# A hybrid attention block on one core: values of three heads projected ahead of the head loop, and each head's last steps placed among the next head's first two weight tiles

## Chip, core and metric

The kernel runs on one core of a Trainium2 chip. The engines are TensorE (PE, with PEld for its weight loads), VectorE (DVE), ScalarE (ACT), GpSimd (POOL) and SyncE (SP), which issues all DMA transfers here. The metric is the device time of one execution in microseconds.

## What is computed

A sequence of 1024 rows of width 1024 is normalised and projected by one weight matrix of 4352 columns. The columns feed three groups of heads; their gated outputs go through one output projection, the residual is added, and the rows are normalised again.

```python
hn = rmsnorm(h, g_norm[l]);  proj = hn @ w_in[l]
aq, ak, av, ag, bq, bk, bv, bg, mq, mg = jnp.split(proj, IN_SPLITS, axis=-1)
# A: 8 query heads of 64, 2 key heads, window of two 64-row chunks, sinks
# B: 4 heads, causal by chunk: softmax(q0 k0) - lam * softmax(q1 k1), times v (128 wide), then rmsnorm
# M: 4 heads of 128 against 256 normalised memory rows
gated = concatenate([a_out * silu(ag), b_out * silu(bg), m_out * silu(mg)])
h = h + gated @ w_out[l];  return rmsnorm(h, g_final)
```

## The kernel before

**Arithmetic.** Every fp32 operand of a product is split into a high part (`hi`, by an ACT copy) and a rest (`lo`, by a subtraction on POOL or DVE). `product` (L1495 to L1499) issues three matmuls, hi by hi, hi by lo and lo by hi. The small A products and all transposes are single fp32 matmuls; a transpose is a matmul against `ident`.

**Stages.** A prologue turns and normalises the memory and the input rows into `x_hi` and `x_lo`, makes keys and values of the memory, and projects the shared keys and values of group A. Then come four heads, written as one list of steps, `HEAD` (L121), and for the last head `LAST`. The output projection ends the kernel.

**A head.** Its eight weight tiles (`TILES`: bk, bq, bv, aq, ag, mq, mg, bg) are 1024 x 128 each. `project(w, s, q)` is a quarter of one half of a tile: six matmuls of 512 columns into bank `acc[:, s]`; four quarters make the half, so a tile takes 48 matmuls. `evacuate(w, s)` empties the bank: for bk with four ACT copies and two DVE subtractions, for bq with two and two, for bv and aq with one DVE instruction, for a gate (ag, mg, bg) with an ACT tanh and a DVE product. The table `BETWEEN` says which attention steps stand behind which quarter; (7, 0, 3) is the last quarter of the first half of tile 7.

**Order and waits.** All five engines walk the same list, each taking its own part of every step, and an engine does its parts strictly in that order. Semaphores join them. A half may start when the bank that it writes was evacuated: `project_quarter` (L1685) waits for `acc_free` of two halves earlier. Transposes go through two banks (`trans`), outputs of attention through one (`mixo`), scores through three (`score`).

**The end of group B in a head.** The squares of the head's output are summed on PE (`b_squares`); `b_finish(s)` takes the root on ACT (L857, which needs another table of functions) and on DVE the reciprocal (L1400) and a product (L1402); `b_gate` (L1410) multiplies by the gates. SP then stores the gates to DRAM (`spill`, L513).

**The values of a head.** Tile bv is projected turned, 128 value columns by 1024 rows, copied to `b_out`, turned back by eight transposes in `v_spread` (L1707), and split to `v_hi` and `v_lo`.

Of the kernel before, what the change touches and what calls it, by code (L numbers as in the profile page):

```python
# [45 lines left out]
TILES = [("bk", BK, True), ("bq", BQ, True), ("bv", BV, False), ("aq", AQ, True),  # L46
         ("ag", AG, True), ("mq", MQ, False), ("mg", MG, False), ("bg", BG, False)]
NT = len(TILES)
BUSY = (14, 2, 2)
PRE_TILES = 10  # L50
MEM_TILES = 8
PRE_RAW = 4
# [5 lines left out]
BETWEEN = {  # L58
    (2, 0, 2): [("b_scores", 0, 0)],
    (2, 0, 3): [("b_scores", 1, 0), ("b_combine", 0)],  # L60
    (2, 1, 1): [("b_combine", 1)],
# [30 lines left out]
}  # L92

def numbered(*events):

    return {key: n for n, key in enumerate(events)}


def head_steps(between):

    out = [("start",)]  # L110
    for w in range(NT):
        out.append(("weights", w + 1))
        for s in range(2):
            for q in range(4):
                out.append(("project", w, s, q))
                if q == 3:
                    out.append(("evacuate", w, s))
                out += between.get((w, s, q), [])
    return out


HEAD = head_steps(BETWEEN)

BETWEEN_LAST = {
    **BETWEEN,
    (7, 1, 0): BETWEEN[(7, 1, 0)] + [("mix_first", 0)],
# [8 lines left out]
LAST = head_steps(BETWEEN_LAST)  # L135
# [15 lines left out]
def score_units():  # L151

    out = []
    for s in HEAD:
# [15 lines left out]
T_AT = numbered(*[s for s in HEAD if s[0] in ("v_spread", "b_spread", "m_spread", "a_spread", "b_squares")])  # L170

T_SPLIT = numbered(*[s for s in HEAD if s[0] in ("v_spread", "b_spread", "m_spread")])

PT_AT = numbered(*[s for s in HEAD if s[0] in ("b_spread", "m_spread")])
PT_MIX = numbered(*[s for s in HEAD if s[0] in ("b_spread", "m_spread")])
assert list(PT_MIX) == [(s[0][0] + "_spread",) + s[1:] for s in HEAD if s[0] in ("b_mix", "m_mix")]
O_AT = numbered(*[s[:2] for s in HEAD
                  if s[0] in ("m_mix", "a_mix") or (s[0] == "b_mix" and s[2] == s[1])])
NS, NTB, NPT, NO = len(S_AT), len(T_AT), len(PT_AT), len(O_AT)
# [5 lines left out]

def build(nc, x, mem, w_in, g_norm, a_sinks, lq1, lk1, lq2, lk2, subln_g, g_mem, w_mem_kv, w_out,
          g_final, y):
    mixed = nc.dram_tensor("mixed", (SPILL_TILES * P, SEQ), F32).ap()

# [6 lines left out]
    mixed_v = mixed.rearrange("(j p) s -> p j s", p=P)  # L196

# [16 lines left out]
    with ctx:  # L214
# [65 lines left out]
        q_m_hi, q_m_lo = q_b[:, 0, :], q_b[:, 1, :]  # L280
        bv_t = b_out[:, 0:SEQ]
        squares = logits[:, 0, 0, :]
# [56 lines left out]
        mixo = ctx.enter_context(nc.psum_tensor("mixo", [P, HALF], F32))  # L339
        y_acc = [score[:, 0, :], score[:, 1, :], trans[:, 0, :], trans[:, 1, :]]  # L340
# [13 lines left out]
        mv_made = sem("mv_made")  # L354
        mem_w_full = [sem(f"mem_w_full{n}") for n in range(2, MEM_TILES)]
# [90 lines left out]
        def raw_at(w, h):  # L446

            return h * (NT // 2 * 32) + 32 * ((PRE_RAW + w) // 2 + 1)


        @block.sync
        def _(sp):
# [49 lines left out]
            for w in range(2):  # L502
                sp.wait_ge(w_lo_done, PRE_TILES - 1 + w)
                load_tile(w_in_v, w, TILES[w][1], 4 * DK)

            def load_head_tile(w, h):

                name, col, two = TILES[w % NT]
                step = DK if two else P
                sp.wait_ge(w_lo_done, at(w - 2, h, NT, PRE_TILES))  # L510
                load_tile(w_in_v, w % 2, h * step + (col + (step if w >= NT else 0)), 4 * DK if two else None)
# [10 lines left out]
            with sp.Fori(0, HEADS - 1) as h:  # L522
                for w in range(2, NT + 2):
                    load_head_tile(w, h)
                for g in "amb":
                    spill(g, h)
            for w in range(2, NT):
                load_head_tile(w, HEADS - 1)

            n_tiles = PRE_TILES + NT * HEADS  # L530

            def load_wo(j):
# [4 lines left out]
                dst = wo_raw[j - 1] if j else w_raw[:, 0, :]  # L537
# [3 lines left out]
                for c, row in enumerate((first, second)):  # L541
                    sp.dma_start(dst[c * DK:(c + 1) * DK, :], w_out_v[row:row + DK, :])\
                      .then_inc(wo_full[j - 1] if j else raw_full[0], 16)
# [11 lines left out]
            for g in "abm":  # L555
                sp.wait_ge(spilled[g], 16 * H)
            sp.wait_ge(mkv_lo, 2 * HEADS)
            load_mix(0, 0)
            sp.wait_ge(s_full, at(S_AT[("b", 7, 1, 1)], H, NS))
            load_wo(1)  # L560
            load_wo(2)
            sp.wait_ge(s_free_dve, len(S_BY_DVE) * HEADS)
            load_mix(1, 1)
            sp.wait_ge(s_full, NS * HEADS)
            load_wo(3)
            sp.wait_ge(acc_full, PRE_ACC + 2 * NT * HEADS)
# [3 lines left out]
            sp.wait_ge(t_free, PRE_T + NTB * HEADS)  # L570
# [923 lines left out]
        def _(pe):  # L1494
# [161 lines left out]
            for v in range(2, 4):  # L1656
                spread_shared(v)
# [252 lines left out]
```

## Time and profile before

| | us |
|---|---|
| median of 3 runs | 703.88 |
| lowest, highest | 703.14, 704.38 |
| the profiled execution | 703.16 |
| its span in the trace | 701.4 |
| PE busy | 691.6 (99%) |
| DVE, ACT, POOL busy | 417.4, 313.2, 231.2 |

A row of the chronological view gives start, duration, engine, line, operation, output and inputs, shape, count, and in brackets the idle time before it and who ended it. Ends of matmuls are modelled and overlap the next one's start, so what PE needs for a matmul is read from start to start. The four heads begin near 65, 190, 314 and 439 us; the output projection runs from 563 us to 696 us.

### The profile page before, as it was taken

How to read it: one execution, taken by the hardware profiler on the slowest of the kernel's cores; microseconds unless marked ns; L12 is line 12 of the kernel's file. 1: busy time of each engine (PE TensorE's matmuls, PEld its weight loads, DVE VectorE, ACT ScalarE, POOL GpSimd, SP SyncE). 2: the span in 40 equal slices, each digit the busy share in tenths (PEclk: the TensorE clock that was granted, in tenths of full speed). 3: DMA queues.
4: the chain of work that ended last, by engine and by line, in shares of the span. 5: the costliest groups of instructions: out<-in, count | busy, mean ns of one | idle time of the engine just before them, and what ended most of it. 6: DMA issues, size and time to landing. Idle time of an engine off the chain costs nothing.

```text
span 701.4 us, 11592 instructions
## 1 busy us (share of the span) xinstructions
PE 691.6 (99%) x3933; PEld 579.2 (83%) x3933; DVE 417.4 (60%) x916; ACT 313.2 (45%) x733; POOL 231.2 (33%) x204
## 2 busy tenths in 40 slices
PE   8999999999999999999999999999999999999996
PEld 8888888888888888888888888888888887888885
DVE  6785246766854666675366667635667786433332
ACT  7763434456543444564344556434464654122200
POOL 5723132234323214433221434323243543222310
PEclk9999999999999999999999999999999999999999
DMA  9921211020052102005211110521140285514210
GB/s 298 310 61 34 57 40 52 1 61 2 1 160 51 55 7 54 8 1 150 61 31 31 32 30 1 150 61 31 31 124 6 60 274 154 158 60 131 84 55 36
DMA packets 79157, 52.73 MB, mean 75 GB/s; under 512 B 36080, under 2 KB 71936, under 8 KB 79104
## 3 DMA queue, kind: packets, MB, share of 16 engines
q1 hardware_dynamic: 79104, 52.06, 26.0%
q8 instruction: 29, 0.48, 0.3%
q14 instruction: 24, 0.20, 0.1%
HBM read 43.14 MB, written 8.91 MB: 74 GB/s over the span
## 4 chain that ended last, share of the span: by engine, by line
PE 92%; DVE 5%; ACT 1%; issue 1%; DVEq 0%; POOL 0%; ACTq 0%; POOLq 0%
PE acc L1497 17%; PE acc L1498 17%; PE acc L1499 17%; PE score L1497 4%; PE score L1498 4%; PE score L1499 4%; PE trans L1498 3%; PE trans L1497 3%; PE trans L1499 3%; PE score L1702 2%; PE score L1704 2%; PE trans L1722 2%; PE mixo L1498 2%; DVE logits L1400 2%; PE mixo L1499 2%; PE mixo L1497 2%
## 5 line engine op out<-in xcount | busy, mean ns | idle before, releaser
L1497 PE MATMUL acc<-x_hi,w_hi 128*128 128x512 f32 x512 | 204.1, 399 | 0.2 <-DVE gates L1265 0.2
L1498 PE MATMUL acc<-x_lo,w_hi 128*128 128x512 f32 x512 | 200.2, 391 | 0.0
L1499 PE MATMUL acc<-x_hi,w_lo 128*128 128x512 f32 x512 | 199.9, 390 | 0.0
L942 POOL TENSOR_TENSOR w_lo<-w_raw,w_hi 128x512 fp32r<-128x512 f32 x66 | 84.9, 1307 | 174.2 <-ACT w_hi L610 156.4
L1499 PEld LDWEIGHTS acc<-x_hi,w_lo 128*128 128x128 f32 x512 | 96.2, 188 | 20.8
L1497 PEld LDWEIGHTS acc<-x_hi,w_hi 128*128 128x128 f32 x512 | 96.3, 188 | 19.3 <-issue 1.4
L1498 PEld LDWEIGHTS acc<-x_lo,w_hi 128*128 128x128 f32 x512 | 96.4, 188 | 16.7
L789 ACT ACTIVATE logits<-logits,stats_b 128x128 f32<-128x128 f32 (+7 forms) x64 | 49.2, 770 | 50.5 <-DVE stats_b L1294 50.5
L1286 DVE CUSTOM_DVE_ANT_0 logits<-score,b_bias 128x384 f32<-128x384 f32 (+5 forms) x96 | 49.8, 554 | 23.2 <-PE score L1704 22.6
L798 ACT ACTIVATE p_hi<-trans 128x512 fp32r<-128x512 f32 (+1 forms) x56 | 30.8, 565 | 63.4 <-PE trans L1722 42.1
L1313 DVE TENSOR_TENSOR p_lo<-trans,p_hi 128x512 fp32r<-128x512 f32 (+1 forms) x56 | 35.8, 651 | 33.6 <-ACT p_hi L798 33.2
L990 POOL TENSOR_SCALAR logits<-logits,stats_b,small 128x128 f32<-128x128 f32 (+7 forms) x32 | 26.3, 823 | 68.1 <-DVE stats_b L1303 68.1
L1306 DVE SCALAR_TENSOR_TENSOR logits<-logits,stats_b 128x128 f32<-128x128 f32 (+7 forms) x32 | 26.2, 818 | 35.4 <-POOL logits L990 35.4
L610 ACT ACTIVATE w_hi<-w_raw 128x512 fp32r<-128x512 f32 x64 | 36.7, 622 | 13.6 <-DMA w_raw<-in_w_in 5.3
L835 ACT ACTIVATE a_band<-a_band,stats_a 128x128 f32<-128x128 f32 x64 | 24.9, 391 | 34.5 <-DVE stats_a L1367 34.2
L965 POOL TENSOR_TENSOR mix_lo<-mix_raw,mix_hi 128x1152 fp32r<-128x1152 f32 (+1 forms) x8 | 18.1, 2260 | 65.6 <-ACT mix_hi L732 64.3
L732 ACT ACTIVATE mix_hi<-mix_raw 128x1152 fp32r<-128x1152 f32 (+2 forms) x10 | 9.6, 971 | 63.2 <-PE score L1499 33.6
L1497 PE MATMUL score<-wo,mix_hi 128*128 128x512 f32 x88 | 34.7, 394 | 0.7 <-DVE wo L1207 0.7
L1498 PE MATMUL score<-wo,mix_hi 128*128 128x512 f32 x88 | 34.3, 389 | 0.0
L1499 PE MATMUL score<-wo,mix_lo 128*128 128x512 f32 x88 | 34.2, 389 | 0.0
L1497 PE MATMUL trans<-wo,mix_hi 128*128 128x512 f32 x88 | 34.2, 389 | 0.0
L1498 PE MATMUL trans<-wo,mix_hi 128*128 128x512 f32 x88 | 34.2, 389 | 0.0
(254 smaller groups left out, 1395.5 us busy)
## 6 DMA issues: line engine op xcount, KB each, us to landing
w_raw<-in_w_in SPq DMA_DIRECT2D x68, 256.0 KB, 3.4
mixed<-gates SPq DMA_DIRECT2D x9, 512.0 KB, 4.2
mix_raw<-mixed SPq DMA_DIRECT2D x8, 576.0 KB, 5.9
wo_raw<-in_w_out SPq DMA_DIRECT2D x8, 512.0 KB, 7.1
x_res<-in_x SPq DMA_DIRECT2D x8, 512.0 KB, 3.3
out_y<-y_row SPq DMA_DIRECT2D x16, 256.0 KB, 2.1
logits<-in_x SPq DMA_DIRECT2D x4, 512.0 KB, 8.0
wo_raw<-in_w_out SPq DMA_DIRECT2D x6, 256.0 KB, 5.9
```

What stands on the lines that cost most here:

```text
L610: act.activation(w_hi[:, slot, cols], w_raw[:, slot, cols], ACT.Copy).then_inc(w_hi_done, 1)
L789: act.activation(logits[:, i % 2, c, 0:width], logits[:, i % 2, c, 0:width], ACT.Exp, bias=b_neg[:, 2 * (i % 2) + c:2 * (i % 2) + c + 1], ...
L798: act.activation(out, trans[:, bank, 0:n], ACT.Copy).then_inc(t_hi, 1)
L835: act.activation(a_band[:, n, :], a_band[:, n, :], ACT.Exp, bias=a_neg[:, n:n + 1], accum_out=a_sum[:, n:n + 1])
L942: last = pool.tensor_tensor(w_lo[:, slot, cols], w_raw[:, slot, cols], w_hi[:, slot, cols].bitcast(F32), ALU.subtract)
L990: pool.tensor_scalar(logits[:, i % 2, 1, 0:width], logits[:, i % 2, 1, 0:width], b_inv[:, 2 * (i % 2) + 1:2 * (i % 2) + 2], neg_lam, ALU.m ...
L1286: dve.tensor_tensor_reduce(out=logits[:, i % 2, c, a:a + n], in0=score[:, unit % S_RING, 0:n], in1=b_bias[:, rel:rel + n], scale=1.0, scal ...
L1306: dve.scalar_tensor_tensor(out=logits[:, i % 2, 0, 0:width], in0=logits[:, i % 2, 0, 0:width], scalar=b_inv[:, k:k + 1], in1=logits[:, i % ...
L1313: dve.tensor_tensor(out, trans[:, T_AT[step] % T_RING, 0:n], hi.bitcast(F32), ALU.subtract)\
L1497: pe.matmul(out, a_hi, b_hi, start=start, stop=False, skip_group_check=True)
L1498: pe.matmul(out, a_hi, b_lo, start=False, stop=False, skip_group_check=True)
L1499: return pe.matmul(out, a_lo, b_hi, start=False, stop=stop, skip_group_check=True)
```

## The change

The four heads keep their arithmetic. The values of heads 0 to 2 are no longer a tile of the head. Four value tiles (numbers 10 to 13) stand between the prologue and head 0: `value_tile` takes the rows of x as the stationary operand and 384 value columns of the weights as the moving one, and makes all eight row blocks in eight banks at once. The result has its rows on the partitions, so that no transpose follows. ACT and DVE copy it out, SP stores it to DRAM (`values`) and loads each head's part back into `b_out`; `v_split` splits it. The keys and values of the memory go through DRAM likewise (`mem_kv`, `mkv`). Head 3 keeps its bv tile.

Heads 0 to 2 have seven tiles. The steps that stood in tile 7 stand in `BEHIND` and are done among tiles 0 and 1 of the next head: `in_order(n)` gives, for turn n, the steps of head n and those left of head n-1. Loops over heads on ACT, DVE, POOL and SP are written out. The memory part's queries get a place of their own. In the last head SP asks for the first `mix_raw` later.

```diff
-TILES = [("bk", BK, True), ("bq", BQ, True), ("bv", BV, False), ("aq", AQ, True),
-         ("ag", AG, True), ("mq", MQ, False), ("mg", MG, False), ("bg", BG, False)]
+TILES = [("bk", BK, True), ("bq", BQ, True), ("aq", AQ, True), ("ag", AG, True), ("mq", MQ, False),
+         ("mg", MG, False), ("bg", BG, False)]
+TILES_LAST = TILES[0:2] + [("bv", BV, False)] + TILES[2:]
...
-    (3, 0, 2): [("b_combine", 3), ("v_spread", 0), ("v_spread", 1)],
+    (2, 0, 0): [("v_split", 0)],
+    (2, 0, 1): [("v_split", 1)],
+    (2, 1, 0): [("mkv",)],
+    (3, 0, 2): [("b_combine", 3)],
...
-    (7, 0, 3): [("m_spread", 3), ("m_mix", 2)],
-    (7, 1, 0): [("a_spread", 3), ("m_mix", 3), ("b_squares", 1)],
-    (7, 1, 1): [("b_finish", 0)],
-    (7, 1, 2): [("b_finish", 1)],
-    (7, 1, 3): [("b_gate",), ("a_mix", 3)],
+BEHIND = {
...
+    (0, 0, 3): [("m_spread", 3), ("m_mix", 2)],
+    (0, 1, 0): [("a_spread", 3), ("m_mix", 3), ("b_squares", 1)],
+    (0, 1, 2): [("a_mix", 3)],
+    (1, 0, 0): [("b_finish", 0)],
+    (1, 0, 2): [("b_finish", 1)],
+    (1, 1, 0): [("b_gate",)],
+}
...
+            def value_tile(n):
+
+                pe.wait_ge(w_lo_done, n + 1)
+                for t in range(ST):
...
+                    for c in range(2):
+                        k = 2 * (n - OWN_TILES) + c
+                        cols = slice(c * HALF, c * HALF + AHEAD)
+                        last = product(v_banks[t][:, 0:AHEAD], x_hi[:, k, rows], x_lo[:, k, rows], w_hi[:, n % 2, cols],
+                                       w_lo[:, n % 2, cols], k == 0, k == KT - 1)
...
+            for h in range(1, HEADS):
+                load_head_tile(2, h)
+                for g in "ma":
+                    spill(g, h - 1)
+                load_mem_kv(h)
+                load_head_tile(3, h)
+                spill("b", h - 1)
+                if h < HEADS - 1:
+                    load_values(h)
...
+                def v_split(half):
+                    ts = slice(4 * half, 4 * half + 4)
+                    act.wait_ge(v_loaded, 16 * (h + 1))
+                    act.wait_ge(pt_done, h * NMIX)
+                    act.activation(v_hi[:, ts, :], v_in[:, ts, :], ACT.Copy).then_inc(v_hi_done, 1)
```

On DVE at the end of a head, before: the gates' half, the last split (`p_lo`), outputs taken from `mixo`, the sums of squares, the four instructions of `b_finish`, the other gates' half, `b_gate`.

```order
L1265 SCALAR_TENSOR_TENSOR gates<-gates,acc 128x512
...
L1313 TENSOR_TENSOR p_lo<-trans,p_hi 128x512
...
L1394 TENSOR_SCALAR logits<-trans 128x512
L1400 RECIPROCAL logits<-logits 128x512
L1402 TENSOR_TENSOR b_out<-b_out,logits 128x512
L1400 RECIPROCAL logits<-logits 128x512
L1402 TENSOR_TENSOR b_out<-b_out,logits 128x512
...
L1265 SCALAR_TENSOR_TENSOR gates<-gates,acc 128x512
L1410 SCALAR_TENSOR_TENSOR gates<-b_out,small,gates 128x512 x2
L1325 SCALAR_TENSOR_TENSOR gates<-mixo,gates 128x256
```

On DVE at the same work now, in tiles 0 and 1 of the next head (`k_lo` is the evacuation of a half of bk, `q_b` of a half of bq).

```order
L1429 TENSOR_TENSOR k_lo<-acc,k_b 64x512 x2
L1497 TENSOR_TENSOR p_lo<-trans,p_hi 128x512
L1508 SCALAR_TENSOR_TENSOR gates<-mixo,gates 128x256
...
L1429 TENSOR_TENSOR k_lo<-acc,k_b 64x512 x2
L1585 RECIPROCAL logits<-logits 128x512
L1587 TENSOR_TENSOR b_out<-b_out,logits 128x512
L1585 RECIPROCAL logits<-logits 128x512
L1587 TENSOR_TENSOR b_out<-b_out,logits 128x512
L1435 SCALAR_TENSOR_TENSOR q_b<-acc,q_b 64x512 x2
L1595 SCALAR_TENSOR_TENSOR gates<-b_out,small,gates 128x512 x2
L1435 SCALAR_TENSOR_TENSOR q_b<-acc,q_b 64x512 x2
```

The split of the last memory step now stands behind a half of bk, and `b_finish` between the second half of bk and the first half of bq.

On ACT at the end of a head, before: tanh of a gates' half, the last `p_hi`, table load, the two roots, table load, tanh of the other half.

```order
L781 ACTIVATE gates<-acc 128x512
...
L798 ACTIVATE p_hi<-trans 128x512
L857 ACT_TABLE_LOAD
L857 ACTIVATE logits<-logits 128x512
...
L857 ACTIVATE logits<-logits 128x512
...
L781 ACT_TABLE_LOAD
L781 ACTIVATE gates<-acc 128x512
```

On ACT now, from the first half of bk (tile 0) of the next head to the first exponentials of its group B.

```order
L934 ACTIVATE k_b<-acc 64x512 x4
L966 ACTIVATE p_hi<-trans 128x512
L934 ACTIVATE k_b<-acc 64x512 x4
L764 ACTIVATE w_hi<-w_raw 128x512 x2
L1025 ACT_TABLE_LOAD
L1025 ACTIVATE logits<-logits 128x512 x2
L938 ACTIVATE q_b<-acc 64x512 x4
L764 ACTIVATE w_hi<-w_raw 128x512 x2
L915 ACTIVATE v_hi<-b_out 128x512 x2
L957 ACT_TABLE_LOAD
```

The roots moved behind the evacuation of a whole bk tile and a weight split, and the split of the values stands in front of the exponentials.

## Rows read from the trace of the kernel before

**Rows 1.** The page, part 1: busy time and share of each engine, and instructions.

```profile
PE 691.6 (99%) x3933; PEld 579.2 (83%) x3933; DVE 417.4 (60%) x916; ACT 313.2 (45%) x733; POOL 231.2 (33%) x204
```

**Rows 2.** Waits of PE, in total, times, longest; all five sum to 3.6 us.

```profile
PE acc L1529 <- POOL ident L928: 1.7, 1, 1.7
```

**Rows 3.** PE in order of time, around `v_spread` of head 1: start, duration.

```profile
228.72 0.39 PE L1497 MATMUL acc<-x_hi,w_hi 128*128 128x512 f32 x1
...
229.40 1.03 PE L1713 MATMUL trans<-ident,b_out 128*128 128x128 f32 x8
230.19 0.48 PE L1497 MATMUL acc<-x_hi,w_hi 128*128 128x512 f32 x1
230.50 0.40 PE L1498 MATMUL acc<-x_lo,w_hi 128*128 128x512 f32 x1
```

**Rows 4.** PE, four score matmuls of 384 columns in a row.

```profile
225.02 0.33 PE L1702 MATMUL score<-k_b,q_b 128*128 128x384 f32 x1
...
225.73 0.40 PE L1497 MATMUL acc<-x_hi,w_hi 128*128 128x512 f32 x1
```

**Rows 5.** ACT, end of head 0 and start of head 1.

```profile
181.02 0.60 ACT L781 ACTIVATE gates<-acc 128x512 f32<-128x512 f32 x1 [1.22 <-PE acc L1499]
181.51 0.59 ACT L798 ACTIVATE p_hi<-trans 128x512 fp32r<-128x512 f32 x1
182.12 1.28 ACT L857 ACT_TABLE_LOAD   x1
183.42 0.63 ACT L857 ACTIVATE logits<-logits 128x512 f32<-128x512 f32 x1
...
190.30 1.14 ACT L610 ACTIVATE w_hi<-w_raw 128x512 fp32r<-128x512 f32 x2
...
200.75 2.44 ACT L769 ACTIVATE k_b<-acc 64x512 fp32r<-64x512 f32 x4 [3.00 <-PE acc L1499]
```

**Rows 6.** DVE, the same stretch.

```profile
182.25 0.68 DVE L1313 TENSOR_TENSOR p_lo<-trans,p_hi 128x512 fp32r<-128x512 f32 x1
182.85 0.41 DVE L1325 SCALAR_TENSOR_TENSOR gates<-mixo,gates 128x256 f32<-128x256 f32 x1
...
185.65 3.34 DVE L1400 RECIPROCAL logits<-logits 128x512 f32<-128x512 f32 x1
...
193.75 0.67 DVE L1265 SCALAR_TENSOR_TENSOR gates<-gates,acc 128x512 f32<-128x512 f32 x1
194.35 1.84 DVE L1410 SCALAR_TENSOR_TENSOR gates<-b_out,small,gates 128x512 f32<-128x512 f32 x2
...
203.22 1.39 DVE L1247 TENSOR_TENSOR k_lo<-acc,k_b 64x512 fp32r<-64x512 f32 x2 [2.90 <-ACT k_b L769]
```

**Rows 7.** PE: `m_mix(3)` of head 0, then tile 2 and `b_spread(0, 0)` of head 1.

```profile
183.71 0.36 PE L1497 MATMUL mixo<-p_hi,mv_hi 128*128 128x256 f32 x1
...
211.46 0.39 PE L1497 MATMUL acc<-x_hi,w_hi 128*128 128x512 f32 x1
...
223.30 0.49 PE L1722 MATMUL trans<-ident,logits 128*128 128x128 f32 x3
```

**Rows 8.** The page, part 6: transfers, count, KB each, median us from issue to landing.

```profile
mixed<-gates SPq DMA_DIRECT2D x9, 512.0 KB, 4.2
mix_raw<-mixed SPq DMA_DIRECT2D x8, 576.0 KB, 5.9
```

**Rows 9.** ACT's last exponential before that `b_spread`, and DVE's instruction behind it.

```profile
219.66 0.49 ACT L789 ACTIVATE logits<-logits,stats_b 128x256 f32<-128x256 f32 x1
221.28 0.48 DVE L1306 SCALAR_TENSOR_TENSOR logits<-logits,stats_b 128x256 f32<-128x256 f32 x1 [0.84 <-POOL logits L990]
```

**Rows 10.** PE's first matmuls; then stretches: busy of each engine, PEclk granted (behind POOL).

```profile
1.72 3.25 PE L1529 MATMUL acc<-ident 128*128 128x128 f32 x14 [1.72 <-POOL ident L928]
...
695.00:697.00 2.00, 0.59 (x3) 0.17 (x1) 1.37 (x3) 0.65 (x2) 0.00 (x0) 1.00 0.00 0
697.00:699.00 2.00, 0.00 (x0) 0.00 (x0) 1.09 (x4) 0.37 (x2) 0.00 (x0) 0.82 0.00 0
```

More of the change, by code:

```diff
@@ new lines, in numbered, with head_steps @@
+def numbered(*events):
+    return {key: n for n, key in enumerate(events)}
+def head_steps(tiles, between):
+    out = [(0, ("start",))]
+    for w in range(len(tiles)):
+        out.append((0, ("weights", w + 1)))
+        for s in range(2):
+            for q in range(4):
+                out.append((0, ("project", w, s, q)))
+                if q == 3:
+                    out.append((0, ("evacuate", w, s)))
+                out += [(0, step) for step in between.get((w, s, q), [])]
+                out += [(1, step) for step in BEHIND.get((w, s, q), [])]
+    return out
@@ new lines, with tiles_of, in_order @@
+HEAD = head_steps(TILES, BETWEEN)
+STEPS = [s for d, s in HEAD if d == 0] + [s for d, s in HEAD if d == 1]
+def tiles_of(h):
+    return TILES_LAST if h == 3 else TILES
+def in_order(h):
+    runs = []
+    for d, s in LAST if h == 3 else HEAD:
+        if d > h:
+            continue
+        if not runs or runs[-1][0] != h - d:
+            runs.append((h - d, []))
+        runs[-1][1].append(s)
+    return runs
+BETWEEN_LAST = {
+    (2, 0, 2): [("b_scores", 0, 0)],
+    (2, 0, 3): [("b_scores", 1, 0), ("b_combine", 0)],
+    (2, 1, 0): [("mkv",)],
@@ L87 @@
     (7, 0, 3): [("m_spread", 3), ("m_mix", 2)],
-    (7, 1, 0): [("a_spread", 3), ("m_mix", 3), ("b_squares", 1)],
-    (7, 1, 1): [("b_finish", 0)],
-    (7, 1, 2): [("b_finish", 1)],
-    (7, 1, 3): [("b_gate",), ("a_mix", 3)],
[L92 to L126, printed above, removed]
+    (7, 1, 0): [("a_spread", 3), ("m_mix", 3), ("b_squares", 1), ("mix_first", 0)],
     (7, 1, 1): [("wo_split", 1)],
@@ L153, in score_units @@
     out = []
-    for s in HEAD:
+    for s in STEPS:
         if s[0] == "b_scores":
@@ L893, in head @@
                         wo_hi_part(s[1])
-            with act.Fori(0, HEADS - 1) as h:
-                head(h, HEAD)
-            head(HEADS - 1, LAST)
+            for n in range(HEADS):
+                for h, order in in_order(n):
+                    head(h, order)
             def finish_row(par, z):
@@ L954, in pre_lo_half @@
                                           ALU.subtract)
-            for n in range(PRE_TILES):
+            for n in range(OWN_TILES):
                 if n > 0:
@@ L1045, in head @@
                             .then_inc(wo_lo_by_pool, 1)
-            with pool.Fori(0, HEADS - 1) as h:
-                head(h, HEAD)
-            head(HEADS - 1, LAST)
+            for n in range(HEADS):
+                for h, order in in_order(n):
+                    head(h, order)
             with pool.Fori(0, ST // 2 - 1) as z:
@@ L1457, in head @@
                         mix_mid_part(s[1])
-            with dve.Fori(0, HEADS - 1) as h:
-                head(h, HEAD)
-            head(HEADS - 1, LAST)
+            for n in range(HEADS):
+                for h, order in in_order(n):
+                    head(h, order)
             def finish(par, z):
@@ L1657, in _ @@
                 spread_shared(v)
+            for n in range(OWN_TILES, PRE_TILES):
+                value_tile(n)
             def head(h, order):
```

363 lines of the change are left out of this document (251 added, 112 removed).

## Prediction

> **What bounds the kernel now.** First the page's busy shares: PE is busy 99% of the span, the other engines 60% or less [rows 1]. Then the list of PE's waits: the longest is the 1.7 us before its first matmul, and all of them together are 3.6 us [rows 2]. So PE sets the end in every stage, and a change pays only by what it takes off PE's own row of work. In exchange, a wait that it puts on PE adds its whole length. Then the order of time on PE, start to start, for the price of its instructions [rows 3, 4], and on ACT and DVE at the seam between two heads [rows 5, 6], because that is where the change puts work. What the reader is to see there is that DVE has 8.1 us of work for `b_finish`, and that PE's next half-tile was released at its very end.
>
> **Part 1, the transposes that go.** `v_spread` of one head holds PE from 229.40 to 230.19, 0.79 us, and the matmul behind it takes 0.31 us to the next start instead of 0.23 [rows 3]: 0.87 us. Three heads lose it: **-2.6 us**, all on PE, so all of it counts.
>
> **Part 2, the value tiles.** Before, three bv tiles are 3 x 48 = 144 matmuls of 512 columns; spaced (229.40 - 228.72)/3 = 0.227 us [rows 3], 32.7 us. Now 4 tiles x 8 row blocks x 2 x 3 = 192 matmuls of 384 columns, as many columns in all. The nearest row has four of that width in (225.73 - 225.02) = 0.71 us, 0.178 each [rows 4]; the other bound takes 128 columns at 2.4 GHz, 0.053 us, off the 512 column spacing: 0.174. That is 33.4 to 34.1 us, +0.7 to +1.4; I take 0.175, **+0.9 us**, because the last spacing in that row runs into another bank. The Trainium skill ("TensorE: Matmul & The Clock Gate", section "Back-to-back issue gap") gives a fixed 2.5 ns above the columns' own time, by which the two would differ by 0.1 us; this trace has 14 ns above it at 512 columns, and the rows decide. Loads, splits and copies of these tiles lie beside 8.4 us of PE work a tile. The copy of one tile's pieces (384 columns on ACT or DVE, two engines in turn) takes less than the 1.05 us that PE needs for a row block, so head 0 finds its first bank empty. If that cover failed, it would cost some 0.5 us once. Head 0's values have a whole bk and bq tile, 21.8 us, to go out and come back. Nothing there is on the path.
>
> **Part 3, the last memory step behind bk.** Count from the moment T at which the half's bank is full, 181.02 [rows 5]. Before, ACT has the tanh and starts `p_hi` at T + 0.49 [rows 5]; DVE ends the split and the gate of `m_mix(2)` at 183.26, and PE reaches `m_mix(3)` at 183.71, T + 2.69, in time [rows 6, 7]. Now the half is bk's: four ACT copies, 2.44 us [rows 5], and two DVE subtractions, 1.39 us, that need all four [rows 6]. DVE is at T + 3.85; the split takes 0.60 to its follower's start and the gate 0.41 [rows 6]: T + 4.9. PE needs both, since `m_mix(3)` reads `p_lo` and writes the bank that the gate reads. It waits 4.9 - 2.7 = 2.2 us. Behind it on PE stands everything else. Three seams: **+6.6 us**. Bounds: 1.8 if ACT's `p_hi` slips into a gap, 2.6 if DVE carries its 1.2 us of bias scaling over into this place.
>
> **Part 4, `b_finish` in front of bq's evacuation.** Count from X, when the second half of bk is full (200.75 in head 1 [rows 5]). PE then does tile 1 and wants tile 2 at 211.46, X + 10.7 [rows 7]; its first half needs bq's first half evacuated. ACT has first the copies of bk (2.44), then the weight split (1.14), the table load (1.28) and the root (0.63) [rows 5]: X + 5.5. DVE then has reciprocal, product, reciprocal, product, in one piece: 185.65 to 193.75, 8.1 us [rows 6]. That is X + 13.6, and only then the two instructions on bq (the shape of `k_lo`, 1.39 [rows 6]): X + 15.0. PE waits 15.0 - 10.7 = 4.3 us. Before, the same 8.1 us started at 185.65, right behind the sums of squares, and its end just met PE. Now the roots stand a tile later in ACT's queue, and DVE's in front of an evacuation with less slack. Three seams: **+12.9 us**. Bounds 3.7 and 5.0 us each, by the table load hidden in ACT's idle time at one end and by products slowed beside POOL at the other.
>
> **Part 5, the values of heads 1 and 2.** Their load goes into `b_out`, so SP asks for it only behind `b_gate` (1.84 us behind bq's evacuation [rows 6], X + 16.8) and behind the store of the gates: X + 17.5. A transfer of 512 to 576 KB lands 4.2 to 5.9 us after its issue [rows 8]: X + 21.7 to 23.4. ACT stands at `v_split` until then, and behind it in its queue are the exponentials. Split 1.14 (two copies of the shape of [rows 5]), table load 1.28, three exponentials of 0.5, then 2.1 us from the last one's start to DVE's end of `b_combine(1)` [rows 9]: X + 27.7 to 29.4. PE wants `b_spread(0, 0)` at X + 15.0 + (223.30 - 211.46) = X + 26.9 [rows 7]. It waits 0.8 to 2.5 us, 1.7 in the middle. Two heads: **+3.3 us**. `mkv` and the new stores hang on nothing that is late; the later first `mix_raw` has some 7 us before ACT asks for it and lands in 5.9 [rows 8]. I cost these at nothing, at most 1 us.
>
> **Part 6, the clock.** PE's last matmul ends at 695.6; the stretch from 697 to 699 has a granted clock of 0.82, so PE was taken from 2.4 to 1.2 GHz some 2.7 us after it stopped [rows 10]. The wait of part 4 is longer than that, the one of part 3 is not. At the lower level the first 14 small matmuls stretch over 3.25 us [rows 10], 0.23 us each where eight of the same shape take 0.79 [rows 3]; a visit to that level of that length costs half of it, 1.6 us. In heads 1 and 2 it is paid out of the wait for the values, which is fixed by DVE's end; in head 3 it is added: **+1.6 us**. The Trainium skill, same page, section "What's actually happening", states that an idle PE is set to the lower level until it is busy again. The trace agrees at both ends of the program. By that rule a kernel that puts long waits on PE pays for them twice; if none of the three long waits meets it, the sum is 1.6 us lower, the first rival.
>
> **Sum.** 703.16 (the profiled execution) - 2.6 + 0.9 + 6.6 + 12.9 + 3.3 + 1.6 = 725.9. The median of the runs lies 0.7 above that execution, so I say **726.0 us**, 3.1% slower.
>
> **The rivals.**
> No fall of the clock in the waits: bq's evacuation may be a little earlier, or PE's waits may not count as idle enough. The same sum without the last term, 724.3 us. For it: no wait of this length stands in the trace. Against it: 2.7 us sufficed at the end.
> A slow return: after each long wait the clock stays low twice as long, 3.2 us a seam, and the waits for values (3.3 us) vanish under it in two heads: 724.3 + 3 x 3.2 - 3.3 = 730.6 us. Against it: the first matmuls of the program were at the higher level after some 3.6 us.
> One of the two seam waits is not there, because an order of semaphores lets PE pass: 726.0 - 6.6 = 719.4 or 726.0 - 12.9 - 3.3 - 1.6 = 708.2. Against it: the rows of the order show both on DVE in front of what PE needs.
> Not slower: DVE is done in time. That needs bq evacuated by X + 10.7, so 4.3 us less between X and there, which would be so if the reciprocals took 1.2 us each and not 3.34, or ACT took its roots in front of bk's copies. Then only parts 1 and 2 count (a later bank release at the seam, 0.2 to 0.4 us today, goes too): 703.2 - 1.7 = 701.5 us. It decides at 4.3 us of DVE and ACT time, and nothing in the rows gives them.
>
> **How the numbers follow.** Forecast with a fall of the clock 0.48; without it 0.30; slow return 0.10; one wait missing 0.07; not slower 0.05. The range: the low end is the case without a fall, with parts 3 and 4 0.4 us a wait shorter (-2.4) and the values at their low bound (-1.7), 720.2, rounded to 719.5 for part 2 and 5's small terms; the high end takes in the slow return, 731. It holds the first two cases and most of the third, some 0.83 once unlisted mishaps are allowed for. A measurement here can tell 0.2% (1.4 us) from no change; faster by more than that 0.04, within it 0.01, slower 0.95.
>
> **What would show it.** Right: three PE waits of some 4.3 us in front of tile 2 of heads 1 to 3, released by DVE's second instruction on `q_b`; three of some 2.2 us in front of `m_mix(3)`, released by DVE's gate; eight transposes of `b_out` instead of 32 at that line; two waits near `b_spread(0, 0)` of heads 1 and 2 with ACT idle until a DMA lands; low clock behind the long waits. Wrong: no PE wait over 1 us in the heads (then parts 3 and 4 fall), or large waits elsewhere, in the value tiles or at the output projection, which I cost at nothing.

## Result and the profile after

The changed kernel takes 733.27 us (median of four runs, 732.93 to 733.67) beside 703.51 us before (702.94 to 704.38): a ratio of 1.042, 95% interval 1.0408 to 1.0432. It is slower, as forecast, but by 29.8 us where 22.5 were forecast, and 2.3 us above the range. The profiled execution took 733.67 us with a span of 731.9 us; before, the span was 701.4 us. These 30.5 us have to be explained.

The page's busy shares, as in [rows 1]. PE's busy time grew by 8 us although it has hardly more to compute, and 32 us of the span are now idle where 10 were.

```profile
PE 699.5 (96%) x3957; PEld 587.8 (80%) x3957; DVE 413.5 (57%) x908; ACT 314.9 (43%) x739; POOL 242.4 (33%) x212
```

PE's waits (what it waited for, total, times, longest), as in [rows 2]. The first two are new: three long ones in front of the third tile of heads 1 to 3, three shorter ones at `m_mix(3)` of heads 0 to 2. The third is the old one at the program's start; the last are the first attention transposes, `b_spread(0, 0)`.

```profile
PE acc L1682 <- DVE q_b L1435: 16.1, 3, 5.4
PE mixo L1682 <- DVE gates L1508: 5.8, 3, 1.9
PE acc L1714 <- POOL ident L1098: 1.7, 1, 1.7
...
PE trans L1938 <- DVE logits L1490: 0.7, 3, 0.3
```

**The short wait.** ACT, DVE and PE in order of time (start, duration) between heads 0 and 1; these answer [rows 5] to [rows 7]. The key half is full at 213.41, DVE has the split and gate done at 218.3, and PE's product follows.

```profile
213.41 2.44 ACT L934 ACTIVATE k_b<-acc 64x512 fp32r<-64x512 f32 x4 [0.54 <-PE acc L1684]
215.88 0.60 ACT L966 ACTIVATE p_hi<-trans 128x512 fp32r<-128x512 f32 x1
```

```profile
215.88 1.39 DVE L1429 TENSOR_TENSOR k_lo<-acc,k_b 64x512 fp32r<-64x512 f32 x2 [2.13 <-ACT k_b L934]
217.31 0.69 DVE L1497 TENSOR_TENSOR p_lo<-trans,p_hi 128x512 fp32r<-128x512 f32 x1
217.91 0.41 DVE L1508 SCALAR_TENSOR_TENSOR gates<-mixo,gates 128x256 f32<-128x256 f32 x1
```

```profile
215.87 0.60 PE L2009 MATMUL trans<-ident,a_probs 128*128 128x128 f32 x4
218.38 0.39 PE L1682 MATMUL mixo<-p_hi,mv_hi 128*128 128x256 f32 x1 [1.92 <-DVE gates L1508]
```

**The long wait.** ACT first (X, the second key half full, is 226.17), then DVE, POOL beside it, and PE. DVE's two reciprocals and two products run from 231.76 to 240.8 in one piece; behind them come the two instructions on `q_b`, and PE resumes at 242.36, X + 16.2.

```profile
226.17 2.44 ACT L934 ACTIVATE k_b<-acc 64x512 fp32r<-64x512 f32 x4 [9.69 <-PE acc L1684]
228.63 1.16 ACT L764 ACTIVATE w_hi<-w_raw 128x512 fp32r<-128x512 f32 x2
229.80 1.28 ACT L1025 ACT_TABLE_LOAD   x1
231.10 1.15 ACT L1025 ACTIVATE logits<-logits 128x512 f32<-128x512 f32 x2
```

```profile
231.76 3.35 DVE L1585 RECIPROCAL logits<-logits 128x512 f32<-128x512 f32 x1 [1.73 <-ACT logits L1025]
235.15 0.69 DVE L1587 TENSOR_TENSOR b_out<-b_out,logits 128x512 f32<-128x512 f32 x1
235.76 3.35 DVE L1585 RECIPROCAL logits<-logits 128x512 f32<-128x512 f32 x1
239.14 1.66 DVE L1587 TENSOR_TENSOR b_out<-b_out,logits 128x512 f32<-128x512 f32 x1
240.83 1.39 DVE L1435 SCALAR_TENSOR_TENSOR q_b<-acc,q_b 64x512 fp32r<-64x512 f32 x2
```

```profile
238.98 2.93 POOL L1112 TENSOR_TENSOR w_lo<-w_raw,w_hi 128x512 fp32r<-128x512 f32 x2 [7.10 <-ACT w_hi L764]
```

```profile
236.62 0.39 PE L1684 MATMUL acc<-x_hi,w_lo 128*128 128x512 f32 x1
242.36 0.77 PE L1682 MATMUL acc<-x_hi,w_hi 128*128 128x512 f32 x1 [5.36 <-DVE q_b L1435]
```

**The clock.** Stretches in us; per engine busy time and count, then the granted clock, DMA share and GB/s (columns as in [rows 10]). In 242 to 247 PE is busy nearly all the time, but with 11 matmuls at 0.51 of the full rate: level 1.2 GHz. 0.81 over five us is a fall 1.9 us before 242, at 240.1, and 0.51 a return near 246.9: 6.8 us low, 4.5 of them with PE at work. The short wait of this seam is followed by it too: 0.57 over 219 to 223 is 3.4 us low, from 219.6 on, when PE had been back at work for 1.2 us. The other two long waits repeat it: 0.52 and 0.54.

```profile
219.00:223.00 4.00, 4.00 (x14) 3.18 (x13) 1.02 (x2) 0.00 (x0) 0.00 (x0) 0.57 0.32 131
...
237.00:242.00 5.00, 0.01 (x1) 0.00 (x0) 4.92 (x4) 2.33 (x4) 2.93 (x2) 0.81 0.00 0
242.00:247.00 5.00, 4.64 (x11) 3.71 (x12) 3.01 (x5) 0.00 (x0) 0.00 (x0) 0.51 0.47 130
247.00:250.00 3.00, 3.00 (x16) 2.51 (x16) 0.67 (x5) 0.82 (x2) 0.11 (x1) 1.00 1.18 314
```

From 242.36 to the transposes at 256.83 PE takes 14.5 us; before, the same stretch took 11.8 [rows 7]. Less the 0.4 us that it waits at the transposes (counted from start to start), **2.2 us** are the price of the half clock behind a long wait.

**Values.** PE, the first and the matmul behind the last of the 192 value matmuls (98.29 - 64.90 = 33.4 us); then, ahead of the transposes in head 1, ACT's split of the values, POOL's first subtraction for `mkv` and its scaling, and DVE. The values were loaded by X + 23.0. Then POOL's two subtractions for `mkv`, 0.7 us each, stand in front of the scaling, and DVE is done at 256.77, X + 30.6.

```profile
64.90 0.42 PE L1682 MATMUL mixo<-w_hi,x_hi 128*128 128x384 f32 x1
...
98.29 0.39 PE L1682 MATMUL acc<-x_hi,w_hi 128*128 128x512 f32 x1
```

```profile
249.18 1.15 ACT L915 ACTIVATE v_hi<-b_out 128x512 fp32r<-128x512 f32 x2 [9.75 <-DMA b_out<-values]
```

```profile
254.20 0.74 POOL L1150 TENSOR_TENSOR mk_lo<-mk_in,mk_hi 128x256 fp32r<-128x256 f32 x1 [0.86 <-ACT mv_hi L909]
...
255.62 0.55 POOL L1166 TENSOR_SCALAR logits<-logits,stats_b,small 128x256 f32<-128x256 f32 x1
```

```profile
256.29 0.48 DVE L1490 SCALAR_TENSOR_TENSOR logits<-logits,stats_b 128x256 f32<-128x256 f32 x1 [2.40 <-POOL logits L1166]
```

**Where the 30.5 us went:** transposes -2.6; value tiles 33.4 - 32.7 = +0.7; short waits 3 x 2.1 = +6.4; long waits 3 x (5.74 - 0.23) = +16.5; half clock behind the long waits 3 x 2.2 = +6.7 and behind one short wait +1.6; the transposes' waits +0.7 by the list, +1.4 if the excess over 0.23 us is counted from start to start in all four heads. That is 30.0 to 30.8. The 1.6 behind the short wait is read between seams: from the transposes ahead of the short wait to the last matmul ahead of the long one PE takes 20.43 us in the first seam and 18.83 in the two others, where the clock stayed up.

### The profile page after: what moved, and what is told of

The parts are those of the page before. It is cut to its first block, busy times and chain, and to the rows that moved or that the text cites. A ratio compares the mean times of both kernels' runs of the same rounds, so it can differ in the third digit from the quotient of the medians.

```text
span 731.9 us, 10888 instructions
## 1 busy us (share of the span) xinstructions
PE 699.5 (96%) x3957; PEld 587.8 (80%) x3957; DVE 413.5 (57%) x908; ACT 314.9 (43%) x739; POOL 242.4 (33%) x212
## 4 chain that ended last, share of the span: by engine, by line
PE 79%; DVE 10%; ACT 5%; issue 3%; POOL 1%; DMA 1%; DVEq 0%; SPq 0%; POOLq 0%; ACTq 0%
PE acc L1682 13%; PE acc L1684 12%; PE acc L1683 12%; PE score L1682 5%; PE score L1684 5%; PE score L1683 5%; DVE logits L1585 4%; PE trans L1684 3%; PE trans L1683 3%; PE trans L1682 3%; PE trans L1938 2%; PE score L1918 2%; PE score L1920 2%; PE mixo L1683 2%; PE mixo L1682 2%
## 5 line engine op out<-in xcount | busy, mean ns | idle before, releaser
L1682 PE MATMUL acc<-x_hi,w_hi 128*128 128x512 f32 x464 | 188.6, 406 | 16.1 <-DVE q_b L1435 16.1
L1683 PE MATMUL acc<-x_lo,w_hi 128*128 128x512 f32 x464 | 184.3, 397 | 0.0
L1684 PE MATMUL acc<-x_hi,w_lo 128*128 128x512 f32 x464 | 184.2, 397 | 0.0
L1112 POOL TENSOR_TENSOR w_lo<-w_raw,w_hi 128x512 fp32r<-128x512 f32 (+1 forms) x68 | 87.8, 1312 | 211.8 <-ACT w_hi L764 169.7
L1682 PEld LDWEIGHTS acc<-x_hi,w_hi 128*128 128x128 f32 x464 | 89.3, 192 | 34.5 <-POOL w_lo L1112 17.2
L1684 PEld LDWEIGHTS acc<-x_hi,w_lo 128*128 128x128 f32 x464 | 88.9, 192 | 19.7
L1683 PEld LDWEIGHTS acc<-x_lo,w_hi 128*128 128x128 f32 x464 | 89.3, 193 | 15.7
L966 ACT ACTIVATE p_hi<-trans 128x512 fp32r<-128x512 f32 (+1 forms) x56 | 30.8, 565 | 61.1 <-PE trans L1938 40.4
L1684 PE MATMUL trans<-wo,mix_lo 128*128 128x512 f32 x88 | 34.2, 389 | 0.0
```

The source lines that it names most:

```text
L966: act.activation(out, trans[:, bank, 0:n], ACT.Copy).then_inc(t_hi, 1)
L1112: last = pool.tensor_tensor(w_lo[:, slot, cols], w_raw[:, slot, cols], w_hi[:, slot, cols].bitcast(F32), ALU.subtract)
L1682: pe.matmul(out, a_hi, b_hi, start=start, stop=False, skip_group_check=True)
L1683: pe.matmul(out, a_hi, b_lo, start=False, stop=False, skip_group_check=True)
L1684: return pe.matmul(out, a_lo, b_hi, start=False, stop=stop, skip_group_check=True)
```

## Experiments

The kernels below change the table `BEHIND` (steps of the head before, by weight tile, half and quarter) or one other thing. The kernel before was run beside each; its median was 703.3 to 703.9 us.

### The square-root step back in the first tile

```diff
+    (0, 1, 1): [("b_finish", 0)],
-    (0, 1, 2): [("a_mix", 3)],
-    (1, 0, 0): [("b_finish", 0)],
-    (1, 0, 2): [("b_finish", 1)],
-    (1, 1, 0): [("b_gate",)],
+    (0, 1, 2): [("a_mix", 3), ("b_finish", 1)],
+    (1, 0, 0): [("b_gate",)],
```

> The two roots, the two reciprocals and their products of the head before stand two to three quarters into the next head's second key half, as in the kernel before, with the gate product at the start of the second tile; the rest is the changed kernel. Theory (the wait of 5.5 us a seam is VectorE reaching the queries' evacuation late because the reciprocals start only after ScalarE's key evacuation, weights and table load): the reciprocals start near 220.5 instead of 231.8 us, VectorE is through before the second key half is full, the wait at the third tile goes in all three seams and with it the half clock behind it: 733.3 - 3 x 5.5 - 3 x 2.3 = 709.9, 708.5 to 711.5, with the waits of 1.9 us at the last memory step left. Rival (VectorE's 8.1 us are simply too much for this stretch wherever they stand): the keys' evacuation is late in their place and PE waits some 2 to 3 us a seam at the second tile's second half: 716 to 722.

Measured: 714.0 us (ratio 1.0142, 1.0126 to 1.0159). The three long waits are gone. PE's waits, and the stretch behind the second short wait:

```profile
PE mixo L1681 <- DVE gates L1507: 5.8, 3, 1.9
...
PE acc L1681 <- DVE k_lo L1428: 1.0, 1, 1.0
```

```profile
336.00:341.00 5.00, 5.00 (x21) 3.73 (x21) 4.57 (x4) 0.63 (x1) 0.00 (x0) 0.66 0.28 108
```

So the place of `b_finish` makes the long wait: 19.3 us of the loss hang on it. The time lies between the two expectations, 4 us above the theory's. Two things make up 2.7 of the 4: the half clock now stands behind two of the short waits where the changed kernel's profile has one (1.6 us), and in the seam that is spared it PE meets DVE's late `k_lo` for 1.1 us from start to start, the rival's mechanism in one seam and at about half its price. The rest is not accounted for.

### The last memory product two quarters later

```diff
-    (0, 1, 0): [("a_spread", 3), ("m_mix", 3), ("b_squares", 1)],
-    (0, 1, 2): [("a_mix", 3)],
+    (0, 1, 0): [("a_spread", 3)],
+    (0, 1, 2): [("m_mix", 3), ("b_squares", 1)],
+    (0, 1, 3): [("a_mix", 3)],
```

> The last memory step's product and the second sum of squares stand two quarters later, the last local product behind the key half; the roots and reciprocals stay as in the changed kernel. Theory (PE waits 1.9 us for the half of probabilities that ScalarE and VectorE take behind the first key evacuation, and only in its place is the clock lost in the first seam): both go, 733.3 - 3 x 2.13 - 1.6 = 725.3, 724 to 727; the wait of 5.4 us at the third tile stays, since it runs from the second key half. Rival (the wait at the third tile is anchored in something that does not come earlier with PE): it grows by what the first wait gives back, and the time stays at 731 to 733.

Measured: 722.8 us (ratio 1.028, 1.0256 to 1.0304). PE's waits:

```profile
PE acc L1683 <- DVE q_b L1436: 10.7, 3, 3.6
PE trans L1939 <- DVE logits L1491: 3.4, 3, 1.6
```

This is 1.2 us under the range. The short waits went, and three things were not in the expectation. First, the long waits shrink from 5.4 to 3.6 us. The local product now lies behind the second key half, so PE wants the third tile at X + 11.5 and not X + 10.7. And DVE ends its part of `q_b` at X + 15.1 and not X + 16.0, because its second product is over before POOL's subtraction begins (DVE, then POOL; X is 222.97 here):

```profile
235.95 0.69 DVE L1588 TENSOR_TENSOR b_out<-b_out,logits 128x512 f32<-128x512 f32 x1
```

```profile
236.63 2.50 POOL L1113 TENSOR_TENSOR w_lo<-w_raw,w_hi 128x512 fp32r<-128x512 f32 x2 [7.93 <-ACT w_hi L765]
```

Second, the clock is low behind each long wait for 3.4 us only (granted 0.57 over 239 to 243). Third, two of the waits at the transposes grew to 1.6 us, which is what part 5 had forecast (1.7): they appear as soon as PE comes to them earlier.

### Both moves

```diff
-    (0, 1, 0): [("a_spread", 3), ("m_mix", 3), ("b_squares", 1)],
-    (0, 1, 2): [("a_mix", 3)],
-    (1, 0, 0): [("b_finish", 0)],
-    (1, 0, 2): [("b_finish", 1)],
-    (1, 1, 0): [("b_gate",)],
+    (0, 1, 0): [("a_spread", 3)],
+    (0, 1, 2): [("m_mix", 3), ("b_squares", 1), ("b_finish", 0)],
+    (0, 1, 3): [("a_mix", 3), ("b_finish", 1)],
+    (1, 0, 2): [("b_gate",)],
```

> Both moves: the last memory product two quarters later, the first root and reciprocal behind it, the second behind the keys' second half, the gate product two quarters into the second tile. Theory: the two waits are apart from each other and both go with their clock: 733.3 - 6.4 - 16.5 - 3 x 2.3 - 1.6 = 701.9, 700.8 to 704, the time of the kernel before less its transposes. Rival (the first reciprocal now stands in front of the keys' second evacuation and the second in front of the queries' first, which both have about 1 us to spare): a wait of 1 to 2 us a seam is left, 705 to 708, more with a fall of the clock.

Measured: 705.6 us (ratio 1.0024, 1.0014 to 1.0033), inside the rival's range and above the theory's. What is left in the seams, from start to start 0.5 us each at the third tile, half of what the rival gave at the least, and 1.8 at the transposes of the four heads together:

```profile
PE acc L1681 <- DVE q_b L1434: 1.1, 3, 0.4
PE trans L1937 <- DVE logits L1489: 0.9, 2, 0.7
```

Of the 29.8 us lost, 27.7 come back by moving six steps by a few quarters of a tile, with no work taken out. The granted clock is 1.00 up to the tail, as no wait in the head loop is over 0.7 us.

### The long wait filled

```diff
+FILL = 24
...
+                        if h > 0 and (w, s) == (2, 0):
+                            pe.wait_ge(t_free, h * NTB + PRE_T)
+                            for _ in range(FILL):
+                                pe.matmul(trans[:, 0, :], x_hi[:, 0, 0:P], x_hi[:, 0, 0:HALF], start=True, stop=True,
+                                          skip_group_check=True)
```

> The changed kernel with 24 matmuls of 512 columns that nobody reads, written to a free bank in front of the wait at the third tile of heads 1 to 3: 24 x 0.227 = 5.4 us of work in a wait of 5.4 us, so the wait is filled and nothing else is moved. Theory (the half clock behind the long waits costs 2.2 to 2.5 us a seam and comes from TensorE standing idle): the granted clock stays at 1.00 through 240 to 247 us and 733.3 - 3 x 2.3 = 726.4, 725 to 728. Rival (what is lost behind the wait is lost on another engine and not by the clock): 733, within 1.

Measured: 735.9 us, with wide scatter (730.6 to 738.4): the expectation of a gain is refuted, and the rival's number is not met either. Two stretches, then PE at the transposes:

```profile
242.00:247.00 5.00, 5.00 (x23) 3.87 (x22) 3.69 (x6) 0.00 (x0) 0.63 (x1) 1.00 0.37 105
...
257.00:261.00 4.00, 3.60 (x11) 3.02 (x12) 1.50 (x3) 1.53 (x3) 1.49 (x2) 0.57 0.00 0
```

```profile
257.40 0.90 PE L1944 MATMUL trans<-ident,logits 128*128 128x128 f32 x3 [2.25 <-DVE logits L1491]
```

The clock theory holds for the place it speaks of: with PE kept busy the clock stays at 1.00. But PE is then 2 us earlier at the transposes, where the values are not ready; it waits 2.3 us in head 1 and 3.0 in head 2 instead of 0.2 and 0.3, and the clock is halved behind these two waits instead (and, in this profile, behind all three short ones).

### The values' split later, without and with the filling

Both move the splits of the values and of `mkv` in the changed kernel (the latter in head 3 too); the second also has the 24 unread matmuls.

```diff
-    (2, 0, 0): [("v_split", 0)],
-    (2, 0, 1): [("v_split", 1)],
-    (2, 1, 0): [("mkv",)],
+    (2, 1, 2): [("v_split", 0), ("v_split", 1)],
+    (3, 1, 0): [("mkv",)],
```

> The changed kernel with its seams as they are; only the splits of the values and of the memory keys and values stand later, as in e8_values_later. Theory (behind a long wait with half clock TensorE reaches the first attention transposes so late that the splits cost it only 0.3 to 0.4 us): 733.3 - (0.28 + 0.40 + 0.44 + 0.35) = 731.8, 730.8 to 732.8, half clock as before behind each long wait. Rival (the splits are what holds TensorE, by the 1.7 us forecast for heads 1 and 2): 729 to 730.

> e11_values_only with the 24 unread matmuls of e5_fill_wait in the long wait. Theory (in e5_fill_wait the filled wait kept the full clock, and what that gave was taken by the new waits of 2.4 and 3.0 us at the first attention transposes, which here have no cause left): no half clock at 240 to 247 us and no wait at the transposes, 731.8 - 3 x 2.3 = 724.9; each half clock that the short waits show beyond the one of the changed kernel adds 1.6: 724 to 728.5. Rival (the filled wait has a price of its own, or what the half clock costs is slack that the next stage needs anyway): 731 and above.

Measured: 731.5 us without (730.1 to 733.0), 726.1 us with (725.1 to 728.4). The stretch behind the first long wait, without and then with filling:

```profile
241.00:245.00 4.00, 3.96 (x10) 3.17 (x11) 2.72 (x4) 0.00 (x0) 0.00 (x0) 0.53 0.46 131
```

```profile
242.00:247.00 5.00, 5.00 (x27) 4.22 (x26) 2.13 (x9) 0.76 (x4) 0.00 (x0) 1.00 0.86 245
```

Both times lie in the ranges of their theories. Neither profile has a wait at the transposes. Filling PE's idle time with work that nobody reads makes the program 5.4 us faster. The theory gives 6.7 less the 1.6 of the one short wait that is followed by a half clock only in the filled kernel's profile: 5.1. So the half clock is a price of its own, and standing idle is its cause.

### A short wait filled

e1_finish_early with nine such matmuls in front of `m_mix(3)`, written to a score bank.

> e1_finish_early with 9 matmuls of 512 columns that nobody reads, written to a free score bank in front of the last memory product of heads 0 to 2: 9 x 0.227 = 2.0 us of work in the wait of 2.1 us that stands there. Theory (the waits of 2.1 us each cost 1.4 us more behind them wherever the clock is halved, two of three in the profile of e1_finish_early, and the halving comes from the idle stretch): no half clock up to the tail, 714.0 - 2 x 1.4 = 711.2, 710.3 to 712.3, and the two waits' own 6.4 us stay. Rival (the halving comes with what the core does at that time and not with TensorE standing idle, or its cost is hidden by a wait further on): 714, within 0.7.

Measured: 714.2 us (ratio 1.0149, 1.0135 to 1.0164), no change from 714.0: the rival's time, by its second branch. PE's waits and the stretch:

```profile
PE acc L1682 <- DVE k_lo L1429: 3.0, 3, 1.0
```

```profile
337.00:341.00 4.00, 4.00 (x31) 3.10 (x31) 3.97 (x3) 0.64 (x1) 0.00 (x0) 1.00 0.33 131
```

The clock stayed up in all three seams, and then PE met the late `k_lo` in all three, 1.1 us each from start to start. With half clock (1.6 us) it lost this wait. Of 1.6 us, 1.1 were slack in front of DVE, so the clock is worth 0.5 us a seam there; over two seams that is as much as the runs of one kernel scatter (713.4 to 714.3).

### POOL kept away from the second product

```diff
+                    if h > 0 and w == 3:
+                        act.wait_ge(acc_free, at(2, h, 2 * NT, PRE_FREE))
                     take_w_hi(slot)
```

> The changed kernel, except that ScalarE's split of the third weight tile of heads 1 to 3 waits for the queries' first evacuation on VectorE, so that GpSimd's 128x1024 subtraction of that tile no longer runs beside the second product of the square-root step. Theory (that product takes 1.66 us instead of 0.69 us because GpSimd works beside it, and the evacuation behind it, which releases TensorE, is late by the difference): the product takes 0.7 us, the wait at the third tile falls from 5.4 to 4.5 us, and 733.3 - 3 x 0.95 = 730.4, 729.5 to 731.5; the half clock behind the wait stays. Rival (the product is long for another reason, or the evacuation takes over what it loses since GpSimd then works beside that): 733, within 0.8.

Measured: 732.1 us (730.6 to 733.7). DVE's second product, and PE's wait:

```profile
239.55 0.69 DVE L1589 TENSOR_TENSOR b_out<-b_out,logits 128x512 f32<-128x512 f32 x1
```

```profile
PE acc L1684 <- DVE q_b L1437: 13.2, 3, 4.4
```

The step of the theory that a trace can show holds: 1.66 us became 0.69 (0.7 expected), the wait of 5.4 became 4.4 (4.5 expected). The time fell by 1.2 us instead of 2.9, to 0.6 us above the theory's range, and the runs overlap those of the changed kernel (732.9 to 733.7). The profile shows two reasons. PE resumes 4.6 us after it ran out of work instead of 5.5, but the clock comes back as late as before: it is low until 247.4 (0.93 granted over 247 to 250), so 5.6 us of the low stretch fall on PE's work and not 4.5. That takes back 0.5 us in each seam. And the half clock stands behind two short waits here (1.6 us more). The stretch, with PE back at work since 241.81:

```profile
242.00:247.00 5.00, 5.00 (x12) 3.91 (x13) 2.49 (x4) 0.93 (x2) 3.00 (x2) 0.50 0.60 174
```

How often the short waits are followed by a half clock in the runs without a profile is not shown.

### Towards a version that gains

e7_reordered moves the first root and reciprocal ahead of the last memory product and the local product behind them; e8_values_later adds the later splits of e11_values_only; e10_local_later moves the local product one more quarter, to (1, 0, 1). The diff is e7_reordered against e3_both_moved.

```diff
-    (0, 1, 2): [("m_mix", 3), ("b_squares", 1), ("b_finish", 0)],
-    (0, 1, 3): [("a_mix", 3), ("b_finish", 1)],
+    (0, 1, 1): [("b_finish", 0)],
+    (0, 1, 2): [("m_mix", 3), ("b_squares", 1)],
+    (0, 1, 3): [("b_finish", 1)],
+    (1, 0, 0): [("a_mix", 3)],
```

> As e3_both_moved, but the first root and reciprocal stand a quarter ahead of the last memory product, the last local product moves behind them into the second tile's first quarter. Theory (what is left in that kernel at the third tile, 0.53 us a seam, is VectorE reaching the queries' evacuation at 232.7 instead of by 232.2 us; the first reciprocal can start at 219.6 instead of 221.5 us): VectorE has 1.5 to 2 us more, the waits go, 705.6 - 3 x 0.53 = 704.0, 703.5 to 704.6. Rival (the gate behind the reciprocal frees the output bank or the squares' bank too late, and a new wait of 0.5 to 2 us stands in its place): 705.5 to 711.

> As e7_reordered, and the splits of the values stand behind the second row block's combination instead of ahead of the first's exponentials, and the split of the memory keys and values half a tile-time later, in all heads. Theory (the waits at the first attention transposes, 0.9, 0.7, 0.35 and 0.3 us in heads 1, 2, 3 and 0, come from ScalarE's values split ahead of the exponentials and GpSimd's memory split ahead of the second scaling): they go, 704.0 - 2.0 = 702.0, 701.4 to 702.8, under the kernel before at 703.75. Rival (the values' transfer, not the splits, is what the transposes wait for, or the splits now hold up the third and fourth row blocks): 703.5 to 705.

> As e8_values_later, with the last local product a quarter later (second tile, second quarter). Theory (what that kernel still waits for between heads, 0.6 us at the local product in three seams, is the gate behind the first reciprocal on VectorE, which ends a quarter of a tile too late): the waits go, 702.9 - 3 x 0.6 = 701.1, 700.6 to 701.9. Rival (the local gate now stands in front of the gate product later and the queries' evacuation is late by that, or the output bank is missed further on): 702.5 to 704.

Measured: 709.9 us (ratio 1.0086, 1.0073 to 1.0099), 702.9 us (0.9989, 0.998 to 0.9998) and 702.0 us (0.9978, 0.9969 to 0.9987). The last two miss their theories' ranges by 0.1 us at most. PE's waits in the first; the second has only the line of `mixo`, with the same numbers, and the third neither, only waits at the program's start and at the output projection.

```profile
PE trans L1939 <- DVE logits L1491: 4.3, 3, 2.2
...
PE mixo L2021 <- DVE gates L1509: 1.3, 3, 0.4
```

e7_reordered lies in the rival's range, but only a part of it is the rival's mechanism, PE waiting at `mixo` for the local gate, 0.6 us a seam from start to start. The larger part neither text has. The waits at the third tile went, but the local gate also releases the store of the gates, and behind that in SP's queue stand the memory keys, the next weights, the last gates and the values. SP's issues, first in e3_both_moved, then here:

```profile
227.40 0.36 SPq L635 DMA_DIRECT2D mixed<-gates  x1
...
233.11 0.43 SPq L651 DMA_DIRECT2D b_out<-values  x1
```

```profile
230.43 0.36 SPq L637 DMA_DIRECT2D mixed<-gates  x1
...
234.53 0.44 SPq L653 DMA_DIRECT2D b_out<-values  x1
```

The load is asked for 1.4 us later, and the transposes wait up to 2.2 us; behind one of these waits the clock is halved too (0.66 over 363 to 368). With the splits out of the way of the exponentials (e8_values_later) no wait is left there. The chain through SP's queue is read from its order in the trace; no run tests it alone.

## The prediction, step by step

**Direction and places: right.** The three waits at `m_mix(3)`, the three at the third tile, the releasers, DVE's order and the low clock behind the long waits are all where the text puts them.

**Parts 1 and 2: right.** 0.174 us a value matmul, the lower bound, so +0.7 and not +0.9. Nothing at the value tiles or the output projection became late. e10_local_later, where of the forecast's terms only these are left, is 1.3 us under the kernel before; the forecast of -1.7 for that case lies in its interval (0.9 to 2.2).

**Part 3: right,** +6.4 for +6.6. That its wait would be too short for the clock was wrong: 1.6 us more in the first seam. The text took the 2.7 us from PE's stop to the fall at the program's end as if they were fixed; here the clock fell 3.1 us after PE stopped in the long wait, and in the short one 1.2 us after PE had resumed.

**Part 4: right in mechanism, a term mis-sized.** DVE's first reciprocal started at X + 5.6 (5.5 forecast). From there the text took 8.1 us as one piece out of the kernel before, where nothing disturbed it; it took 9.07, since POOL's `w_lo` of the tile to come, released by ACT at just that time, ran beside the second product (1.66 for 0.69 us; e6_weights_wait shows the cause), and PE came 0.14 us behind DVE. 16.5 for 12.9, and over the upper bound of 5.0 a wait, which had named this slowing but priced it too low.

**Parts 5 and 6: the step that failed most.** The text has 3.3 for the values and 1.6 for the clock, 4.9 together; measured are 0.7 and 8.3, 9.0 together. Two errors. The visit to the low clock was priced by the program's start, half of 3.25 us. (The granted clock reads 1.00 there; what shows the low level are the starts of the small matmuls, 0.21 us apart up to 5.4 us and 0.11 from then on.) Behind a long wait it lasted from 240.1 to 246.9, and the last 4.5 us of it fell on PE's work: 2.2 us, not 1.6, and in all three seams. And the lateness was set against the wait in one direction only. PE came to the transposes later than forecast by part 4's 1.2 and the clock's 2.2 us. That covered the values' wait and left the rest as loss: the text let the clock vanish under this wait, while this wait vanished under the clock. The wait itself is real: e2_mix_later shows 1.6 and e5_fill_wait 2.3 us once PE comes in time. It was even larger than the 1.7 us of the text, because `mkv`, put at nothing there, was on its path: from the start of ACT's last exponential, 252.92, to DVE's end it took 3.9 us and not the 2.1 of [rows 9], as POOL's two subtractions stood between. DVE was done at X + 30.6, not X + 27.7 to 29.4. In the changed kernel PE's lateness hid nearly all of it.

With part 4 at +3.6 and parts 5 and 6 at +4.1, and 0.4 less for parts 2 and 3, the sum of 22.7 becomes 30.0. The sum has a slip too: 725.9 is built on the profiled execution of 703.16 us, and with the 0.7 us by which the median lay above it, it is 726.6 and not 726.0. The rivals "no fall of the clock" and "not slower" are refuted; "slow return" had the right mechanism for the high end, at a lower price than it gave, but it was added to a part 4 that was itself too small. The range's upper end missed because it took one cause at its worst and not two together.

The Trainium skill ("TensorE: Matmul & The Clock Gate", section "What's actually happening") states that the engine is set to the lower level while idle and raised when it is busy again. e11_values_only (0.53 granted over 241 to 245) and e12_values_fill (1.00 over 242 to 247) agree on the fall, and the 5.4 us between them price it. On the way back the traces show that the full rate does not come with the first matmul: PE worked 4.5 us at 1.2 GHz.

**Open:** a short wait of 2.1 us is followed by a half clock in some seams and not in others, and not in the same ones from profile to profile: first seam here, first and second in e6_weights_wait, second and third in e1_finish_early, second in e12_values_fill, all three in e5_fill_wait, none in e11_values_only. What decides it no run here tells apart.

## What to carry to other kernels

When steps of one stage are pushed into the next, count each queue behind them from the moment that releases it: the same 8 us of DVE work cost nothing where ACT's roots released it in time, and 16.5 us in three seams where ACT came to them behind a key evacuation, a weight split and a table load. Price a wait on PE with its clock: here a long one of 5.5 us cost 2.2 us more, and one of 4.6 us (e6_weights_wait) 2.8 more, so that the time gained is less than what the wait lost in length. And a lateness hides the waits behind it: taking one away (e5_fill_wait, e9_fill_short, e7_reordered) brings the next to light, so look for that next wait before forecasting the gain.

## What the runs showed that was not expected

- Unread matmuls in a wait made a program faster, 731.5 to 726.1 us, and in another with a wait behind it gave nothing (714.0, 714.2).
- The clock fell behind waits of 2.1 us (low for 3.4 us, 0.57 granted over 219 to 223) as well as behind those of 5.4 us (low for 6.8 us).
- A DVE product of 128x512 took 1.66 us beside POOL's subtractions and 0.69 without them (e6_weights_wait, e2_mix_later); POOL's pair took 2.93 us where it took 2.54 elsewhere. POOL's first subtraction here lasts 1.26 us:

```profile
238.98 1.26 POOL L1112 TENSOR_TENSOR w_lo<-w_raw,w_hi 128x512 fp32r<-128x512 f32 x1 [7.10 <-ACT w_hi L764]
```

It began 0.16 us ahead of the product and ended at 240.24; the product ended 0.56 us later, as if nearly all of it had run behind it. The Trainium skill ("SBUF — State Buffer", section "SBUF: two separate sides") states that a DVE instruction with two inputs in SBUF and a GpSimd instruction that reads SBUF take the shared port in turn, whoever starts first keeping it to its end. These rows agree; the product has two such inputs. No run here tells that lock from a slowing of both.
